# Rotation tables built during attention, residual and norm by row block, and a gather over four PSUM banks

## What is computed

```python
def _rmsnorm(x, g):
    y = xf * lax.rsqrt(jnp.mean(xf * xf, axis=-1, keepdims=True) + EPS)
    return (y * g).astype(x.dtype)
# for each layer L
h = _modulate(_rmsnorm(x, norm_mix_g[L]), shift, scale)
x = x + gate * mixer(h)      # L=0: attention | RG-LRU; L=1: S5 scan + GLU
h = _modulate(_rmsnorm(x, norm_ffn_g[L]), shift, scale)
x = x + gate * hier_moe(h)   # top-1 group, top-2 experts of it
# at the end
out = _rmsnorm(x, final_g)
# in the S5 mixer: h_t = a * h_{t-1} + b_t, a complex for each state,
# and a**t enters as tables of cosines and sines (the rotation tables)
```

## Time and profile before

| | us |
|---|---|
| median of 3 runs | 915.39 |
| lowest and highest | 914.74, 916.45 |
| the profiled execution, its own time | 917.71 |
| its span, first to last instruction | 916.0 |
| PE busy | 843.4 (92%) |
| DVE, ACT, POOL busy | 310.6, 190.6, 167.6 |
| moved by DMA | 285.32 MB, mean 311 GB/s |

### The profile page before, as it was taken

One profiled execution on the slowest core, in us unless ns is written; L12 is line 12 of the kernel. 1 busy time (PEld: TensorE's weight loads), 2 busy tenths in 40 slices (PEclk: granted clock), 3 DMA queues, 4 the chain that ended last, 5 costly groups with the idle time before them and its releaser, 6 DMA issues.

```text
span 916.0 us, 12808 instructions
## 1 busy us (share of the span) xinstructions
PE 843.4 (92%) x5255; PEld 453.5 (50%) x5256; DVE 310.6 (34%) x694; ACT 190.6 (21%) x310; POOL 167.6 (18%) x258
## 2 busy tenths in 40 slices
PE   3899999989999998989689999789999899999993
PEld 1377644655464643644546544434444554654641
DVE  1547233571221500631699510621000311312315
ACT  1402331411311311311500100410001212213111
POOL 2301010398434343510023100000000000000000
PEclk9999999999999999989889999989999999999997
DMA  9999999569999999996996892206866299999991
GB/s 328 329 381 309 387 362 368 201 231 398 395 397 400 396 396 400 395 392 240 390 370 246 288 355 92 92 2 215 312 242 246 96 391 395 392 399 390 397 375 70
DMA packets 126288, 285.32 MB, mean 311 GB/s; under 512 B 7092, under 2 KB 8388, under 8 KB 125992
## 3 DMA queue, kind: packets, MB, share of 16 engines
q1 hardware_dynamic: 123552, 277.88, 82.3%
q0 software_dynamic: 1984, 5.21, 1.9%
q10 hardware_dynamic: 712, 1.67, 0.5%
HBM read 279.50 MB, written 5.24 MB: 311 GB/s over the span
## 4 chain that ended last, share of the span: by engine, by line
PE 78%; DMA 9%; DVE 7%; SPq 4%; issue 1%; ACT 1%; DVEq 0%; ACTq 0%
PE PS L1614 17%; PE PS L1633 12%; PE PS L1641 8%; PE PS L1657 7%; PE PS L1919 6%; PE PS L1617 6%; DMA ring<-in_moe_w 5%; PE PS L1383 3%; PE PS L1455 3%; PE PS L1572 3%; PE PS L1353 3%; SPq L341 2%; DMA ring<-in_ab_w_in 2%; DMA ring<-in_ada_w 2%; DVE work L1198 2%; PE PS L1438 2%
## 5 line engine op out<-in xcount | busy, mean ns | idle before, releaser
L1633 PE MATMUL PS<-ring,work 128*64 128x512 f32 (+1 forms) x512 | 128.6, 595 | 0.3 <-DMA ring<-in_moe_w 0.3
L1614 PE MATMUL PS<-ring,hT 128*64 128x256 f32 x896 | 112.4, 395 | 4.6 <-DMA ring<-in_moe_w 4.6
L1614 PE MATMUL PS<-ring,yg 128*64 128x256 f32 x896 | 107.6, 383 | 0.0
L1219 DVE TENSOR_TENSOR work<-work,PS 128x512 f32<-128x512 f32 x32 | 22.0, 686 | 197.9 <-PE PS L1614 149.7
L1614 PEld LDWEIGHTS PS<-ring,hT 128*64 128x64 f32 x896 | 64.0, 141 | 47.9 <-issue 12.8
L1614 PEld LDWEIGHTS PS<-ring,yg 128*64 128x64 f32 x896 | 65.2, 139 | 33.9 <-issue 2.2
L1641 PE MATMUL PS<-work,xhat 128*128 128x256 f32 (+1 forms) x256 | 74.7, 440 | 7.9 <-issue 7.3
L1633 PEld LDWEIGHTS PS<-ring,work 128*64 128x64 f32 (+1 forms) x512 | 42.9, 143 | 74.9 <-issue 71.9
L1223 DVE COPY yg<-PS 128x512 f32<-128x512 f32 x32 | 22.1, 691 | 145.3 <-PE PS L1633 145.3
L1657 PE MATMUL PS<-yg,grow 64*128 64x512 f32 (+1 forms) x256 | 68.0, 606 | 0.0
L1641 PEld LDWEIGHTS PS<-work,xhat 128*128 128x128 f32 x256 | 46.8, 198 | 38.4 <-issue 22.0
(11 more groups left out here) (353 smaller groups left out, 983.7 us busy)
## 6 DMA issues: line engine op xcount, KB each, us to landing
ring<-in_moe_w SPq DMA_DIRECT2D x96, 2048.0 KB, 17.8
ring<-in_ada_w SPq DMA_DIRECT2D x20, 2048.0 KB, 17.6
work<-in_ada_w SPq DMA_DIRECT2D x4, 2048.0 KB, 15.9
ring<-in_s_glu_w SPq DMA_DIRECT2D x4, 2048.0 KB, 16.4
ring<-in_ab_w_in SPq DMA_DIRECT2D x3, 2048.0 KB, 25.6
ring<-in_ab_w_out SPq DMA_DIRECT2D x2, 2048.0 KB, 21.2
rot_tables<-work POOLq DMA_DIRECT2D x16, 256.0 KB, 5.7
ring<-rot_tables SPq DMA_DIRECT2D x2, 2048.0 KB, 10.9
```

Source lines behind the costliest of these rows:

```text
L1219: v.tensor_tensor(he[:, e % 2, :], he[:, e % 2, :], bank[1], ALU.mult).then_inc(S("he_ready"), 1)
L1614: last = mm(dst[64 * u:64 * u + 64, 0:256], hg[k][:, e * P:e * P + 64], w[:, k, 256 * u:256 * u + 256], start=k == 0, stop=k == KD - 1)
L1633: last = mm(dst, left[:, at:at + (64 if narrow else P)], w[:, c4, h * HALF:(h + 1) * HALF], start=c4 == 0, stop=c4 == KF - 1)
```

## The change

Three edits come together.

**The rotation tables move.** POOL now computes `E2`, `E1` and the rotation tables right after the small loads, as soon as `s5c_ready` has come, ahead of the loads of the S5 input matrices and of the memsets. The halves with cosines and those with sines have a tile each, `rot_st[0]` and `rot_st[1]`, and a semaphore each (`rot_out0`, `rot_out1`); both tiles are the two halves of `grow`. ACT's first `gate_row`, which writes `grow`, waits for all 16 transfers.

**Residual and norm go by row block.** A helper `add_rows` signals when rows 0 are complete (`x_rows0`) and when the low half of rows 1 is (`x_rows1_lo`). ACT squares rows 0 and takes their root while DVE still adds rows 1; the squares of rows 1 are halved between ACT and DVE; ACT scales rows 0, DVE rows 1. The reciprocal for rows 0 stands on DVE ahead of the last add. In the final norm the weights `final_g` are multiplied in with the scaling, and their load is issued earlier. The first `keep_busy` of a router has one product in place of four.

**The gather uses banks 0 to 3.** Block `k` waits for the evacuation of block `k - 4`.

```diff
+            pool.wait_ge(S("s5c_ready"), 1)
...
+            for k in range(KD):
+                    stage = rot_st[v]
+                    if k:
+                        pool.wait_ge(S(f"rot_out{v}"), 16 * k)
+                    g.tensor_tensor(t4(stage), outer(p1), inner(p2), ALU.mult)
+                    ch.link(g.tensor_tensor(t4(rtmp), outer(p3), inner(p4), ALU.mult))
+                    ch.link(g.tensor_tensor(stage, stage, rtmp, op))
+                    pool.dma_start(rot_d[:, k, v, :], stage).then_inc(S(f"rot_out{v}"), 16)
-            pool.wait_ge(S("xr_ps"), 2)
...
             def gate_row(n):
                 act.wait_ge(S("grow_ps"), n + 1)
+                if n == 0:
+                    for v in range(2):
+                        act.wait_ge(S(f"rot_out{v}"), 16 * KD)
...
+                ch.link(s.activation(xhat[:, 0, :], x[:, 0, :], ACT.Square, accum_out=stat[:, 0:1]))
+                s.activation(stat[:, 4:5], stat[:, 0:1], ACT.Sqrt, scale=1.0 / D, bias=stat[:, 2:3]).then_inc(
+                    S("std0_ready"), 1)
+                    act.wait_ge(S("x_rows1_lo"), n)
+                ch.link(s.activation(xhat[:, 1, 0:HALF], x[:, 1, 0:HALF], ACT.Square, accum_out=stat[:, 1:2]))
+                    act.wait_ge(S("rstd0_ready"), n + 1)
+                    s.activation(xhat[:, 0, :], x[:, 0, :], ACT.Copy, scale=stat[:, 6:7]).then_inc(S("xhat0_ready"), 1)
...
+            def add_rows(r, b, h, tmp):
+                if (b, h) == (1, 1):
+                    first_rstd(r)
+                done = v.tensor_tensor(x[...], x[...], tmp, ALU.add)
+                if (b, h) == (0, 1):
+                    done.then_inc(S("x_rows0"), 1)
+                if (b, h) == (1, 0):
+                    done.then_inc(S("x_rows1_lo"), 1)
...
-                keep_busy(6, 4)
+                keep_busy(6, 1)
...
+                            if k == 2:
+                                pe.wait_ge(S("grow_ready"), 2 * L + 2)
+                                pe.wait_ge(S("y_act"), 1 + e0)
+                                pe.wait_ge(S("y_dve"), 1 + e0)
+                            if k >= 4:
+                                pe.wait_ge(S(("hg_act", "hg_dve")[k % 2]), 4 * gi + k // 2 - 1)
+                            gather_block(k, narrow, k % 4).then_inc(S("gathered"), 1)
```

More of the change, by code:

```diff
@@ new lines, in _ @@
+            for table, steps in ((E2, (1, 2, 4, 8)), (E1, (1, 2, 4))):
+                Ec, Es = table[:, 0, :, :], table[:, 1, :, :]
+                g.memset(Ec[:, :, 0:1], 1.0)
+                ch.link(g.memset(Es[:, :, 0:1], 0.0))
+                for n_ in steps:
+                    c_b = w32(0).unsqueeze(2).to_broadcast([P, NQT, n_])
+                    s_b = w32(1).unsqueeze(2).to_broadcast([P, NQT, n_])
+                    te = [Et[:, m, 0:NQT * n_].rearrange("p (q n) -> p q n", n=n_) for m in range(2)]
+                    g.tensor_tensor(te[0], Ec[:, :, 0:n_], c_b, ALU.mult)
+                    ch.link(g.tensor_tensor(te[1], Es[:, :, 0:n_], s_b, ALU.mult))
+                    ch.link(g.tensor_tensor(Ec[:, :, n_:2 * n_], te[0], te[1], ALU.subtract))
+                    g.tensor_tensor(te[0], Ec[:, :, 0:n_], s_b, ALU.mult)
+                    ch.link(g.tensor_tensor(te[1], Es[:, :, 0:n_], c_b, ALU.mult))
+                    ch.link(g.tensor_tensor(Es[:, :, n_:2 * n_], te[0], te[1], ALU.add))
+                    g.tensor_tensor(w32(2), w32(0), w32(0), ALU.mult)
+                    g.tensor_tensor(w32(3), w32(1), w32(1), ALU.mult)
+                    ch.link(g.tensor_tensor(w32(4), w32(0), w32(1), ALU.mult))
+                    g.tensor_tensor(w32(0), w32(2), w32(3), ALU.subtract)
+                    ch.link(g.tensor_scalar(w32(1), w32(4), 2.0, None, ALU.mult))
@@ L1100, in _ @@
             mod_scale(2)
-            def residual(n, waits, psum):
-                dve.wait_ge(S("grow_ready"), n + 1)
-                tmp = xhat[:, 0, :].rearrange("p (h n) -> p h n", h=2)
-                for b in range(NB):
-                    for h in range(2):
-                        dve.wait_ge(S(waits), (2 * b + h + 1) + 4 * (n // 2))
-                        gr = grow[:, h * HALF:(h + 1) * HALF]
-                        link(v.tensor_tensor(tmp[:, h, :], psum(b, h), gr, ALU.mult))
-                        last = v.tensor_tensor(x[:, b, h * HALF:(h + 1) * HALF], x[:, b, h * HALF:(h + 1) * HALF],
-                                               tmp[:, h, :], ALU.add)
-                return last
-            residual(0, "m_ps", lambda b, h: bank[2 * b + h]).then_inc(S("x_new"), 1)
-            dve.wait_ge(S("x_new"), 1)
+            def add_rows(r, b, h, tmp):
+                if (b, h) == (1, 1):
+                    first_rstd(r)
+                done = v.tensor_tensor(x[:, b, h * HALF:(h + 1) * HALF], x[:, b, h * HALF:(h + 1) * HALF], tmp, ALU.add)
+                if (b, h) == (0, 1):
+                    done.then_inc(S("x_rows0"), 1)
+                if (b, h) == (1, 0):
+                    done.then_inc(S("x_rows1_lo"), 1)
+                if (b, h) == (1, 1):
+                    done.then_inc(S("x_new"), 1)
+                    dve.wait_ge(S("x_new"), r)
+            dve.wait_ge(S("grow_ready"), 1)
+            for b in range(NB):
+                for h in range(2):
+                    tmp = xhat[:, 1, h * HALF:(h + 1) * HALF]
+                    dve.wait_ge(S("m_ps"), 2 * b + h + 1)
+                    link(v.tensor_tensor(tmp, bank[2 * b + h], grow[:, h * HALF:(h + 1) * HALF], ALU.mult))
+                    add_rows(1, b, h, tmp)
             def ffn(L):
@@ L1267, in ffn @@
                         link(v.tensor_tensor(tmp[:, h, :], acc[2 * b + h], gfrow[:, h * HALF:(h + 1) * HALF], ALU.mult))
-                        last = v.tensor_tensor(x[:, b, h * HALF:(h + 1) * HALF], x[:, b, h * HALF:(h + 1) * HALF],
-                                               tmp[:, h, :], ALU.add)
-                last.then_inc(S("x_new"), 1)
-                dve.wait_ge(S("x_new"), 2 * L + 2)
+                        add_rows(2 * L + 2, b, h, tmp[:, h, :])
             ffn(0)
@@ L1335, in _ @@
                 link(v.tensor_tensor(q_a[:, m, :], q_a[:, m, :], grow[:, h * HALF:(h + 1) * HALF], ALU.mult))
-                last = v.tensor_tensor(x[:, b, h * HALF:(h + 1) * HALF], x[:, b, h * HALF:(h + 1) * HALF], q_a[:, m, :],
-                                       ALU.add)
-            last.then_inc(S("x_new"), 1)
-            dve.wait_ge(S("x_new"), 3)
+                add_rows(3, b, h, q_a[:, m, :])
             ffn(1)
             norm(4)
-            dve.wait_ge(S("fg_in"), 16)
-            for b in range(NB):
-                v.tensor_tensor(xhat[:, b, :], xhat[:, b, :], fing, ALU.mult).then_inc(S("out_ready"), 1)
         @block.tensor
```

147 lines of the change are left out of this document (63 added, 84 removed).

## The result

| | before | changed |
|---|---|---|
| median of 4 runs | 915.29 us (914.74 to 916.45) | 927.99 us (926.00 to 930.27) |
| ratio, 95% interval | | 1.0138 (1.0110 to 1.0165) |
| profiled execution's own time, span | 917.7, 916.0 | 930.3, 928.5 |

The change makes the kernel 12.7 us slower. The forecast was 6.1 us slower, with a range of 912 to 931. The direction was right, the size was half of what came.

What follows compares the result with a forecast made beforehand. The experts were taken as bound by streaming weights over DMA, the norms by a chain of small steps. Terms 22.5 - 12.3 - 0.9 - 1.1 + 0.3 - 2.4 = +6.1 us gave 923.8 profiled, 921.5 median; range 912 to 931.

Steps and rivals of the forecast that it cites:

- the moved tables: Layer 0: gate row 24.5 us later, experts 11.4 shorter through moved table work; +13.1 us together.
- the rest: Row-block residual and norms, final norm, and four-bank gather: together -7.0 us.
- The tables' end: POOL ahead of layer 0's gate row: tables complete at 174.4 us, including 3 us of contention with DVE.
- The bounds: Delay of POOL's table work beside DVE's long two-input operations: between no cost and 17 us; 3 taken.
- The stop in group 3: End of layer 0's experts: `H0` no longer delays group 3's picks, so the residual follows sooner; -4.2 us.
- The end of the experts: Layer 0's residual would begin 9.1 us behind the last byte, as in layer 1, instead of 13.3.
- The collision of `H0` with the picks: Group 0 of layer 0's experts: POOL's `H0` slows DVE's picks and PE waits; +3.4 us, between 0 and 5.5.
- The norms and the end: Residual and norms in both layers, and the final norm: terms totalling -5.2 us.
- The loads of the condition: Ahead of layer 0's gate row: table writes delay conditioning loads by up to 10.6 us, costed at nothing.
- the tables are held further: Rival: DVE or slower transfers delay the tables by 8 to 14 us more; 929 to 936 us, chance 0.14.
- Early tables: Rival: last table transfer lands near 165 with transfers under 4.4 us, experts' gain whole; 909 to 913 us, chance 0.15.
- an even trade: Rival: tables end near 170 and half the picks collision happens; 914 to 917 us, chance 0.13.

Runs made afterwards that it cites:

- t_only: The kernel before with only the rotation tables moved, including the gate row's wait for them; 936.05 us, ratio 1.0238.
- the repeat: The changed kernel itself, unaltered, profiled and timed once more with later experiments; median 928.34 us, ratio 1.0138.
- short_tables: The changed kernel without the arithmetic of the last two of eight pairs of table halves and their transfer waits; 912.41 us.
- g_only: The kernel before with only the gather through four banks; 914.00 us, ratio 0.9985.
- n_only: The kernel before with only the residual and norms by row block, including the shorter `keep_busy`; 909.62 us, ratio 0.9938.
- gn_only: The changed kernel with the rotation tables put back where the kernel before computes them; 905.30 us, ratio 0.9911.
- hold_memset: gn_only with POOL's last three memsets moved behind the router's product; 908.40 us.
- b_late: The changed kernel with POOL's b tables and `H0` kept back until the picks of group 1 are made; 923.68 us, ratio 1.0082.
- free_gate: The changed kernel with layer 0's gate row in `gfrow`, table waits moved to the first use of `grow` as `pickT`; 913.68 us, ratio 0.9978.

## Why the prediction was right and wrong

The mechanism was right: the gate row waits for the tables, and the stage hangs on it. Two steps of the sum failed: the end of the tables, and the term for the stop in group 3 together with the way from the profiled execution to the median. The forecast put the moved tables at 24.5 - 11.4 = +13.1 us, and t_only measured +19.8; the rest (-7.0) was as put.

- **The tables' end, put at 174.4: measured 178.8, and 178.0 in the repeat.** POOL started 1.4 later than put (62.75 for 61.3); in the repeat `s5c` came as before, so this is mostly the spread between executions. The powers took 1.0 longer. The halves took 81.05 for 76: the pairs 9.8 and not 9.6 (1.3 over seven), the rest lengthened operations. With the powers, contention is near 5 us and not 3. The bounds were 0 and 17; I chose near the lower one, thinking that POOL would mostly be waiting for a transfer when DVE's long operations fell. That assumption failed, and the sum beside it could have shown it: a pair of 9.6 us with 8.8 of work leaves 0.8 for waiting, 5.6 in all. The waits came to 6.6, and of the 6.0 us by which the operations of the halves were longer, 3.8 reached the end. Landing (5.1) was as put. The size was off by 3.6 to 4.4 us, and by short_tables each of them counts in full.
- **The stop in group 3, put at -4.2.** It was the difference of two ends, 13.3 and 9.1 us behind the last byte. The 13.3 (13.0 by finer windows) belongs mostly to one execution: four kernels with `H0` in the same place (g_only, n_only, gn_only, hold_memset) have 9.4 to 10.6. What was left to win on the median is near zero. And the sum was then lowered by 2.3 once more, to come from this slow execution to the median: the same excess was taken off twice, once as a gain of the change and once as a trait of the execution. On the execution's own scale the forecast was 923.8, and what came is 4.2 above it. That the 2.3 sit just there is argued, from the 3 us by which this end differs and from the intervals of n_only and g_only, not measured.
- **The end of the experts, put at 9.1 behind the last byte:** 10.0 and 9.9. The row was from layer 1, and layer 0 has this microsecond without any POOL beside it (9.9 in b_late).

These are 3.6 to 4.4, 2.3, and 0.8 to 0.9, together 6.7 to 7.6. The forecast missed by 6.6.

The collision of `H0` with the picks was as put, as far as the sum shows it: in t_only the last byte comes 241.2 us behind the gather and in before 248.4, so 7.2 were won, and the terms (-10.6 and +3.4) give 7.2. That the two agree to the tenth is chance.

What held: the gate row waits for the tables (an idle time of over 25 us was put, 37.0 came), with the residual, the norm and the router behind it. In the changed kernel the last byte comes 241.3 us behind the gather, 239.7 in the repeat (240 put). The norms and the end gave 6.0 (5.2 put). The loads of the condition, pushed back by the writes, were costed at nothing, and in free_gate the gate row is as early as before; that the B matrices had left this part helped, and was not in the forecast.

Of the rivals, "the tables are held further" comes nearest in the time (929 to 936), but asked for 8 to 14 us more from the tables alone, and 4 came. By the rule of the Trainium skill, page "SBUF — State Buffer", section "Who interferes with whom", that was weighed there, the hold was put at up to 17. About 5 came at POOL, and most of the rest fell on DVE (last section). "Early tables" and "an even trade" fall: the tables did not end near 165 or 170. Their transfers took over 5 us, not under 4.4, and an undisturbed pair still waited 1.1 to 1.5 us for one. A chance of 0.72 for slower was right. The forecast's own span of 918 to 926 was too narrow for terms that are each read from a single execution.

## What to carry to other kernels

Work that is moved off the end of a stage costs nothing only as long as nobody waits for the buffer that it borrows: here a free tile for staging tied the gate row to POOL's 111 us of table work. Borrow a tile whose next writer comes late, or give that writer another tile, as free_gate did with `gfrow`. Then look for what the wait had hidden: removing it gave 15 us, and moving what stood behind it on POOL (the memsets, the B loads, the b tables and `H0`) 12 more. A gain that is read as the difference of two stretches of one trace needs a second execution, and must not be counted again when the sum is brought to the median.

## What the runs showed of the hardware

- **POOL's instructions hold DVE's TENSOR_SCALAR.** Eight picks (TENSOR_SCALAR, 128x128) take 1.66 us alone and 6.15 beside POOL's long operations, eight weighted ones 2.13 and 9.11, or 0.8 and 1.1 each, up to about one POOL operation. TENSOR_TENSOR and TENSOR_REDUCE on 128x40 elements beside memsets stayed at 0.20. The Trainium skill, page "SBUF — State Buffer", section "Who interferes with whom", has both: `tensor_scalar` can take the port pair that DVE shares with GpSimd, and a GpSimd instruction that only writes does not hold one with two inputs. The traces agree with both. What the section does not tell is when a hold spans more than one instruction, as with the 128x4 operation that outlasted five (8.21 us).
- **Two-input operations hold each other, and both engines pay.** Beside the tables DVE's four scans took 5.11 us and the product behind them 3.47, against 2.44 and 1.22 in the kernel before, and POOL's operations up to 2.34 for 1.27. All such DVE operations from 84 to 142 us took 28.8 us for 17.5 before, 11.3 more; POOL's took 6.0 more in the halves and 1.0 in the powers. Together that is 18, about the 17 us of overlap that the forecast took as its upper bound. So mutual exclusion fits the sum, and the error of that bound was to put all of it on POOL. What fell on DVE cost the gate row 2 us at most (149.67 to 151.98 in the four kernels without the wait, 149.84 before).
- **A full share is not a full stream.** Beside the same loads of the B matrices the kernel before moved only 286 and 125 GB/s at a share of 1.09 and 1.05, in the two windows from 80 to 88 us, where the windows from 60 to 80 have 382 to 388:

```profile
80.00:84.00 4.00, 4.00 (x23) 3.54 (x20) 3.87 (x9) 0.12 (x1) 0.00 (x0) 1.00 1.09 286
84.00:88.00 4.00, 4.00 (x27) 2.76 (x29) 3.82 (x10) 3.48 (x4) 0.00 (x0) 1.00 1.05 125
```

The change had moved them to 174 to 185, where the stream was running out. The forecast had not seen this. Whether it won time no run shows: without the wait (free_gate) the gate row stands where it stood before.
